# Output projection by halves of the tokens, with the first half's norms beside the second half, in a two-layer FP32 trunk

## The chip, the cores and the metric

One core of a Trainium2 chip runs the whole kernel. The metric is the device time of one execution in microseconds, as the median of several. Five engines work on their own queues and wait for each other through semaphores: TensorE (PE; matmuls and weight loads), VectorE (DVE), ScalarE (ACT), GpSimd (POOL) and SyncE (SP, which only issues DMAs here). Each engine works its instructions off in order.

## The reference

A trunk of two layers over 1024 tokens of width 1024, in FP32. The changed part is what stands between an attention and the up projection of the feed-forward, twice, and the first steps of that:

```python
a = attention_output @ w_o                       # (1024, 1024) @ (1024, 1024)
x = x + rmsnorm(a, g_attn_post[layer])
h = rmsnorm(x, g_ffn_pre[layer])
u = h @ w_up                                     # 1024 -> 2 * 2816
u = causal_conv3(u) + conv_b                     # per channel, over tokens
gate, val = split(u)
f = (silu(gate) * val) @ w_down
x = x + rmsnorm(f, g_ffn_post[layer])
```

## The kernel before

**Layout and precision.** Everything lies transposed: 128 channels on the partitions, tokens along the row. A `128x1024` tile is 128 channels of all tokens, and a *half* is 512 of its columns, so 512 tokens; `half_of(t, k, half)` is such a half of tile k. The width of 1024 makes KT = 8 tiles, 2816 hidden channels make HT = 22 hidden tiles. Every FP32 product is made of three matmuls in fp32r: with each operand split into a high part (a cast) and a low part (the rest), W·X is hi·hi + hi·lo + lo·hi. The weights' parts are made by GpSimd (`split`, two instructions, for the attention's weights; `item` for those of the feed-forward), the activations' by ScalarE (high) and VectorE (low). A product of 128 channels for 512 tokens over eight input tiles is 24 matmuls and fills one PSUM bank; there are eight banks.

**Output projection** (`out_product` on each engine). Units are pairs of weight tiles; for each unit (128 output channels) TensorE makes both token halves, in banks 0 to 3 (`pair_of_units`). VectorE copies each bank to `a`, ScalarE squares it, VectorE adds the square to `ss` (L1754). Loops (`Fori`) run over pairs of units. GpSimd splits a unit's weights when TensorE is through with the ones in their place.

**Norms behind it.** `a_stats` sums `ss` over the partitions by a matmul with ones (L852); ScalarE makes 1/rms with Ln and Exp (L1166, L1168). `x_norm(1)` scales each half tile (L1551), adds it to `x` (L1555, two of three of them on GpSimd, `norm_help`, L718), ScalarE squares it (L1211) and TensorE sums 16 squares (`x_stats`, L845). Then `blocks` makes the feed-forward's input: scaling (L1534), high part (L1175), low part (L1529). `x` is spilled to memory by ScalarE's queue since the room is needed.

**The feed-forward.** Hidden tiles 0 and 1 are plain: products g0, g1, v0, v1 (gate or value, token half 0 or 1), in banks 0 to 3 for both tiles (`plain`, L1080 to L1082). From tile 2 on seven half-size products P1 to P7 stand for eight (Strassen's scheme in Winograd's form; `product`, L1109 to L1111), on sums of weights (S1 to S4, GpSimd) and sums of blocks of the input (T1 to T4), which VectorE makes once in the head of the feed-forward (`sums_of` L1777, `sum_rests` L1783; ScalarE's `sum_tops`, L1186). They use banks 0 to 3; the down projection (`down`, L1127 to L1129) uses banks 4 to 7, and VectorE adds its tiles to `a` (`add`, L1824 for the first hidden tile, L1827). The convolution is one step on ScalarE (`tap`, L1425) and two on VectorE (`conv_tile`, L1804 and L1807); then comes silu (L1429), the product with the value (L1813), and the two parts of `hid` (L1431, L1817).

**What sets the order.** The order on each engine is written out; `STEPS` is TensorE's (`tensor_steps`), `ITEMS` GpSimd's (`weight_items`), and `plan_ring` gives each item one of five places, the one that comes free first. Before, TensorE's order in the head is: plain tile 0 as g0, v0, g1, v1; tile 1 as g0, g1, v0, v1; P1 and P2 of tile 2; the eight down tiles of hidden tile 0; P6, P5, P7, P4 and so on. P1 and P2 write the banks that the convolutions of tile 1 read, and wait for these.

## Time and profile before

| what | us |
|---|---|
| median of 3 runs (2713.6 to 2719.74) | 2714.56 |
| the profiled execution | 2718.21 |
| its span, first to last instruction | 2716.4 |
| TensorE busy in it (matmuls) | 2493.6 |
| VectorE busy in it | 1967.2 |
| mean granted clock of TensorE | 0.967 of full |

The profile is of one execution. Times count from the start of its span. The end of a matmul is modelled, so neighbouring ones overlap on paper; the distance between two starts is the reliable number. "Idle before" an instruction is followed by what ended it. PEclk is the granted clock of TensorE as a share of the full 2.4 GHz; at the lower of its two levels, 1.2 GHz, it is 0.50.

### The profile page before, as it was taken

Reading aid. Unit: us, or ns where it says so; the run is one execution under the profiler, and the core shown is the slowest. Engines: PE = TensorE matmul, PEld = TensorE weight load, DVE = VectorE, ACT = ScalarE, POOL = GpSimd, SP = SyncE. Lnnn points to the kernel's source line nnn. Section 1 sums busy time; section 2 is a strip of 40 time slices with the busy share of each in tenths; the row PEclk is TensorE's granted clock in tenths of the full one; section 3 lists DMA queues with packets and bytes.
Section 4 is the critical chain, followed back from the end, with each engine's and each line's share of the span. In section 5 each row is a group of like instructions: output and inputs, shape, how many; then the busy total and the mean of one; then the engine's idle time right before and its main releaser. Section 6 shows DMA issues by size and latency. Waiting matters only on the chain.

```text
span 2716.4 us, 31720 instructions
## 1 busy us (share of the span) xinstructions
PE 2493.6 (92%) x11964; PEld 1971.9 (73%) x11964; DVE 1967.2 (72%) x2181; ACT 827.7 (30%) x1409; POOL 1490.1 (55%) x1153
## 2 busy tenths in 40 slices
PE   7999999879999999996899999979889999999994
PEld 4688888557777777773577787857467777777772
DVE  4466674586888878889766677653687888788878
ACT  3344442241111111113346565651331111111112
POOL 4231212446888888884431323112537888888883
PEclk9999999999999999998999999979989999999997
DMA  3121223111111111113211213042211111111112
GB/s 133 48 76 63 70 94 149 68 62 47 47 47 55 62 47 47 55 40 144 66 49 45 70 61 86 20 154 93 75 50 47 47 55 57 53 47 48 53 55 116
DMA packets 48928, 183.52 MB, mean 68 GB/s; under 512 B 5648, under 2 KB 6160, under 8 KB 45072
## 3 DMA queue, kind: packets, MB, share of 16 engines
q1 hardware_dynamic: 36880, 140.53, 16.1%
q10 hardware_dynamic: 11904, 41.05, 3.9%
q8 instruction: 93, 1.52, 0.2%
q14 instruction: 51, 0.42, 0.0%
HBM read 138.04 MB, written 29.36 MB: 62 GB/s over the span
## 4 chain that ended last, share of the span: by engine, by line
PE 74%; DVE 16%; ACT 4%; issue 2%; DMA 2%; SPq 1%; ACTq 0%; POOL 0%; POOLq 0%; DVEq 0%
PE ps L1109 9%; PE ps L1110 9%; PE ps L1111 9%; PE ps L1127 6%; PE ps L1129 5%; PE ps L1128 5%; PE ps L975 3%; PE ps L873 3%; PE ps L874 3%; PE ps L875 3%; PE ps L947 2%; DVE a L1551 2%; PE ps L949 2%; PE ps L948 2%; PE ps L1012 2%
## 5 line engine op out<-in xcount | busy, mean ns | idle before, releaser
L1827 DVE TENSOR_TENSOR a<-a,ps 128x1024 f32<-128x1024 f32 x336 | 409.2, 1220 | 173.4 <-PE ps L1129 165.7
L702 POOL CAST w_hi<-w_raw 128x1024 fp32r<-128x1024 f32 x62 | 68.2, 1100 | 648.9 <-PE ps L949 275.3
L785 POOL TENSOR_TENSOR ring<-w_raw,ring 128x512 fp32r<-128x512 f32 x216 | 315.8, 1462 | 17.3
L1425 ACT ACTIVATE cy<-cx,cv 128x1024 f32<-128x1024 f32 x80 | 99.7, 1246 | 718.7 <-DVE cx L1798 718.7
L1127 PE MATMUL ps<-hid,ring 128*128 128x512 f32 x704 | 294.1, 418 | 14.7 <-DVE a L1827 13.5
L783 POOL CAST ring<-w_raw 128x512 fp32r<-128x512 f32 x216 | 176.9, 819 | 235.6 <-PE ps L1129 100.0
L1129 PE MATMUL ps<-hid,ring 128*128 128x512 f32 x704 | 277.1, 394 | 0.0
L1128 PE MATMUL ps<-hid,ring 128*128 128x512 f32 x704 | 276.9, 393 | 0.0
L1109 PE MATMUL ps<-h,ring 128*128 128x512 f32 x640 | 253.3, 396 | 22.1 <-DVE cy L1807 22.1
L1110 PE MATMUL ps<-h,ring 128*128 128x512 f32 x640 | 252.2, 394 | 0.0
L1111 PE MATMUL ps<-h,ring 128*128 128x512 f32 x640 | 252.0, 394 | 0.0
L1127 PEld LDWEIGHTS ps<-hid,ring 128*128 128x128 f32 x704 | 132.5, 188 | 101.1 <-DVE a L1827 64.8
L1798 DVE TENSOR_TENSOR cx<-cx,ps 128x512 f32<-128x512 f32 x280 | 186.9, 680 | 21.8 <-PE ps L1111 13.2
L1109 PEld LDWEIGHTS ps<-h,ring 128*128 128x128 f32 x640 | 122.1, 191 | 49.5 <-issue 24.0
L1129 PEld LDWEIGHTS ps<-hid,ring 128*128 128x128 f32 x704 | 132.9, 189 | 29.9
L704 POOL TENSOR_TENSOR w_lo<-w_raw,w_hi 128x1024 fp32r<-128x1024 f32 x62 | 151.9, 2449 | 5.0
L785 POOL TENSOR_TENSOR ring<-raw_d,ring 128x512 fp32r<-128x512 f32 x88 | 147.2, 1673 | 7.1
L1128 PEld LDWEIGHTS ps<-hid,ring 128*128 128x128 f32 x704 | 133.1, 189 | 20.3
L783 POOL CAST ring<-raw_d 128x512 fp32r<-128x512 f32 x88 | 132.9, 1510 | 26.4 <-PE ps L1082 11.2
L873 PE MATMUL ps<-h,w_hi 128*128 128x512 f32 x352 | 139.8, 397 | 8.3 <-POOL h L723 4.3
L1804 DVE SCALAR_TENSOR_TENSOR cy<-cx,cv,cy 128x1023 f32<-128x1023 f32 x80 | 145.8, 1823 | 0.0
L1111 PEld LDWEIGHTS ps<-h,ring 128*128 128x128 f32 x640 | 122.1, 191 | 26.1
(229 smaller groups left out, 6517.0 us busy)
## 6 DMA issues: line engine op xcount, KB each, us to landing
w_raw<-in_W SPq DMA_DIRECT2D x150, 512.0 KB, 3.5
raw_d<-in_W SPq DMA_DIRECT2D x44, 512.0 KB, 3.5
h<-o_dram ACTq DMA_DIRECT2D x2, 6144.0 KB, 21.0
x_dram<-x ACTq DMA_DIRECT2D x6, 2048.0 KB, 7.2
x<-x_dram SPq DMA_DIRECT2D x2, 4096.0 KB, 12.9
dsw<-draw SPq DMA_DIRECT2D x64, 128.0 KB, 2.3
o_dram<-most SPq DMA_DIRECT2D x6, 1024.0 KB, 4.2
o_dram<-dost SPq DMA_DIRECT2D x6, 1024.0 KB, 4.7
```

Of the source, the lines that this page charges most:

```text
L704: pool.tensor_tensor(w_lo[:, slot, :], w_raw[:, slot, :], w_hi[:, slot, :].bitcast(F32), ALU.subtract).then_inc(w_split, 1)
L783: pool.tensor_copy(half_of(at_, 0, 0), raw[name]).then_inc(item_hi, 1)
L785: pool.tensor_tensor(half_of(at_, 0, 1), raw[name], half_of(at_, 0, 0).bitcast(F32), ALU.subtract).then_inc(item_ready, 1)
L873: pe.matmul(out, wh, xh, start=k == 0, stop=False)
L1109: pe.matmul(out, wh, xh, start=k == 0, stop=False)
L1110: pe.matmul(out, wh, xl, start=False, stop=False)
L1111: last = pe.matmul(out, wl, xh, start=False, stop=k == KH - 1)
L1127: pe.matmul(out, wh, xh, start=True, stop=False)
L1128: pe.matmul(out, wh, xl, start=False, stop=False)
L1129: last = pe.matmul(out, wl, xh, start=False, stop=True)
L1798: dve.tensor_tensor(dst, src, up_bank(n, product), ALU.add).then_inc(c_sum, 1)
L1827: dve.tensor_tensor(a[:, f, :], a[:, f, :], src, ALU.add).then_inc(acc_done, 1)
```

## The change

The projection goes over the first 512 tokens with all eight weight tiles, then over the second 512 with all eight again, so that each weight tile is loaded and split twice (`U_WO = 2 * KT`, and the host lays `w_o` out twice). It uses two banks in turn. The loops are written out. The first norm, the addition to `x`, the second norm and the blocks of the first half (`out_norms` on ScalarE, `new_x` and `blocks` on VectorE) are placed among the steps of the projection's second half; those of the second half come behind it. The 1/rms values stay in the PSUM banks where the sums were made, and so do the scaled tiles on their way; the blocks of the first half are made in PSUM and ScalarE copies them to `a` as well (`b_kept`). All additions to `x` are VectorE's. TensorE's sums are placed between units and, for the second half (`STAT_PLACES`), inside the plain products.

In the feed-forward, TensorE makes the first token half of both plain tiles, then the second half of both; tile 1 uses banks 4 to 7 (`bank(4 * n + ...)`). The weights of tile 1 go to room in `h` (`BESIDE`) instead of the ring. P6 and P5 of tile 2 are moved ahead of the down tiles of tile 0; those are copied to `a` by ScalarE (`first_sum`) instead of VectorE. The order of the convolutions and sums on VectorE and ScalarE changes with it.

```diff
-U_WO = KT
+U_WO = 2 * KT
...
+    out = [("up", n, c) for half in "01" for n in range(PLAIN) for c in ("g" + half, "v" + half)]
     for n in range(PLAIN, HT):
         ups, tiles = [("up", n, c) for c in PRODUCTS], [("dn", n - 1, f) for f in range(KT)]
         if n == PLAIN:
-            first = [("up", n, "P1"), ("up", n, "P2")]
-            out += first + [("dn", m_, f) for m_ in range(n - 1) for f in range(KT)]
-            ups = [u for u in ups if u not in first]
+            out += [("up", n, c) for c in ("P1", "P2", "P6", "P5")] + [("dn", 0, f) for f in range(KT)]
+            ups = [("up", n, c) for c in ("P7", "P4", "P3")]
         if n == HT - 1:
             out += ups + tiles
         else:
...
-    free = {r: (-1 if r < RING - 1 else -2, None) for r in range(RING)}
+    free = {r: (n - RING, None) for n, r in enumerate((4, 0, 2, 1, 3))}
     slot, after = {}, {}
     for it in ITEMS:
+        if it[0] == 1 and it[1] in BESIDE:
+            continue
...
+        STAT_PLACES = {(0, 1, KT - 1): (0, 1), (1, 0, 0): (1, 2), (1, 0, 4): (2, 4), (1, 1, 0): (4, 6), (1, 1, 3): (6, 7),
+                       (1, 1, 6): (7, KT)}
...
+                    if n <= PLAIN:
+                        sp.wait_ge(item_ready, item_count(layer, n - 1, "G2"))
+                        load_ffn(layer, n, "G")
                         sp.wait_ge(item_ready, item_count(layer, n - 1, "V2"))
                         load_ffn(layer, n, "V")
...
                 u0, ch = UNIT0[name], CH[name]
-                for u in range(2):
-                    split(u, u0 + u, before[u])
-                with pool.Fori(1, KT // 2) as q:
-                    free = pairs_free(ch, q - 1)
-                    for u in range(2):
-                        split(u, u0 + 2 * q + u, free[u])
-                return pairs_free(ch, KT // 2 - 1)
+                for u in range(U_WO):
+                    split(u % 2, u0 + u, before[u] if u < 2 else (proj_done, ch + u - 1))
+                return [(proj_done, ch + U_WO - 1), (proj_done, ch + U_WO)]
...
-                pe.wait_ge(proj_out, CH[name])
-                pair_of_units(UNIT0[name], CH[name], True, None)
-                with pe.Fori(1, KT // 2) as q:
-                    pair_of_units(UNIT0[name] + 2 * q, CH[name] + 4 * q, False, None)
+                u0, ch = UNIT0[name], CH[name]
+                for half in range(2):
+                    for t_ in range(KT):
+                        n = KT * half + t_
+                        pe.wait_ge(w_split, u0 + n + 1)
+                        pe.wait_ge(proj_out, ch + n - 1 if n >= 2 else ch)
+                        for k in range(KT):
+                            wh, wl = blk(n % 2, k)
+                            xh, xl = half_of(h, 2 * k, half), half_of(h, 2 * k + 1, half)
+                            pe.matmul(bank(n % 2), wh, xh, start=k == 0, stop=False)
+                            pe.matmul(bank(n % 2), wh, xl, start=False, stop=False)
+                            last = pe.matmul(bank(n % 2), wl, xh, start=False, stop=k == KT - 1)
+                        last.then_inc(proj_done, 1)
+                        if n == KT:
+                            pe.wait_ge(ss_add, SQ0[name] + KT)
+                            a_sum(0)
+                        elif n in (KT + 2, KT + 3):
+                            x_sums(2 * layer + 1, 0, 3 * (n - KT - 2), 3 * (n - KT - 1))
+                        elif n == KT + 4:
+                            x_sums(2 * layer + 1, 0, 6, KT)
...
+                    out = bank(4 * n + 2 * v + half)
+                    if (n, part) == (0, "g0"):
+                        pe.wait_ge(proj_out, CH[f"wo{layer}"] + U_WO)
+                        pe.wait_ge(b_kept, KT * (layer + 1))
                     for k in range(KT):
+                        if (n, part, k) == (0, "g0", 6):
+                            pe.wait_ge(b_lo, 2 * KT * layer + KT)
+                            pe.wait_ge(ss_add, SS[2 * layer])
+                            a_sum(1)
+                        if half == 0 and (n, v, k) in STAT_PLACES:
+                            x_sums(2 * layer + 1, 1, *STAT_PLACES[n, v, k])
...
-                    if n > 0 or f >= 2:
-                        pe.wait_ge(acc_done, down_count(layer, n, f) - 2)
+                    if n == 0 and f < 2:
+                        pe.wait_ge(conv_done, conv_count(layer, 1, f))
+                    elif KT * n + f < KT + 2:
+                        pe.wait_ge(acc_first, KT * layer + KT * n + f - 1)
+                    else:
+                        pe.wait_ge(acc_done, acc_count(layer, n, f) - 2)
                     f4 = f % 4
...
+            def out_norms(layer):
+
+                ch, c0, na, nx = CH[f"wo{layer}"], SQ0[f"wo{layer}"], 2 * layer, 2 * layer + 1
+
+                def square(n):
+                    act.wait_ge(proj_out, ch + n + 1)
+                    if n >= 2:
+                        act.wait_ge(ss_add, c0 + n - 1)
+                    act.activation(half_of(sq, 1, n % 2), half_of(a, n % KT, n // KT), ACT.Square).then_inc(a_sq, 1)
...
+                def x_square(i):
+                    half, k = NORM_TILES[i]
+                    act.wait_ge(f_new, 16 * layer + i + 1)
+                    if i >= 2:
+                        act.wait_ge(x_stat, nx * 16 + i - 1)
+                    act.activation(half_of(sq, 0, i % 2), half_of(x, k, half), ACT.Square).then_inc(x_sq, 1)
+
...
+                def block_parts(i):
+
+                    half, k = NORM_TILES[i]
+                    src = half_of(a, k, half) if half else block_bank(i)
+                    act.wait_ge(b_f, 2 * KT * layer + i + 1)
+                    act.activation(direct(half, k)[0], src, ACT.Copy).then_inc(b_hi, 1)
+                    if half == 0:
+                        act.activation(half_of(a, k, half), src, ACT.Copy).then_inc(b_kept, 1)
+
+                for n in range(KT):
+                    square(n)
+                rstd_a(0)
+                square(KT)
+                for n, squares in enumerate(((0, 1), (2, 3, 4), (5, 6, 7))):
+                    for i in squares:
+                        x_square(i)
+                    if n == 2:
+                        spill(0)
+                    square(KT + n + 1)
+                square(KT + 4)
+                rstd_x(0)
+                for n, tiles_ in enumerate(((0, 1, 2), (3, 4, 5), (6, 7))):
+                    for i in tiles_:
+                        block_parts(i)
+                    square(KT + 5 + n)
+                rstd_a(1)
+                for i in range(KT, 2 * KT):
+                    x_square(i)
+                spill(1)
+                rstd_x(1)
+                for i in range(KT, 2 * KT):
+                    block_parts(i)
...
+                def first_sum(f):
+
+                    act.wait_ge(dn_done, down_count(layer, 0, f))
+                    for c in (("T1", "T3") if f < KH else ("T4",)):
+                        act.wait_ge(t_rest[c], KH * layer + f % KH + 1)
+                    act.activation(a[:, f, :], bank(4 + 2 * (f % 2), 2), ACT.Copy).then_inc(acc_first, 1)
...
                 sum_tops(layer, "T2")
-                gate_and_split(1)
+                sum_tops(layer, "T1")
+                gate(1)
+                sum_tops(layer, "T3")
+                sum_tops(layer, "T4")
+                for f in range(KT - 1):
+                    first_sum(f)
                 bank_copy(layer, PLAIN)
+                first_sum(KT - 1)
+                hid_top(1)
...
+                def copy(n):
+                    dve.wait_ge(proj_done, ch + n + 1)
+                    dve.tensor_copy(half_of(a, n % KT, n // KT), bank(n % 2)).then_inc(proj_out, 1)
+
+                def add_square(n):
+                    dve.wait_ge(a_sq, q0 + n + 1)
+                    dve.wait_ge(ss_add, c0 + n)
+                    dve.tensor_tensor(half_of(ss, 0, n // KT), half_of(ss, 0, n // KT), half_of(sq, 1, n % 2),
+                                      ALU.add).then_inc(ss_add, 1)
+
+                def new_x(i):
+                    half, k = NORM_TILES[i]
+                    if k == 0:
+                        dve.wait_ge(a_rstd, 2 * na + half + 1)
+                    if k >= 2:
+                        dve.wait_ge(f_new, 16 * layer + i - 1)
+                    dve.scalar_tensor_tensor(added_bank(half, i), half_of(a, k, half), gain(post, k), bank(4 + half),
+                                             ALU.mult, ALU.mult).then_inc(a_normed, 1)
+                    dve.wait_ge(a_normed, na * 16 + i + 1)
+                    dve.tensor_tensor(half_of(x, k, half), half_of(x, k, half), added_bank(half, i), ALU.add
+                                      ).then_inc(f_new, 1)
...
+                def block(i):
+                    half, k = NORM_TILES[i]
...
+                    dve.scalar_tensor_tensor(half_of(a, k, half) if half else block_bank(i), half_of(x, k, half),
+                                             gain(pre, k), bank(6 + half), ALU.mult, ALU.mult).then_inc(b_f, 1)
...
+                    if half:
+                        dve.wait_ge(b_hi, 2 * KT * layer + i + 1)
+                    else:
+                        dve.wait_ge(b_kept, KT * layer + i + 1)
+                    dve.tensor_tensor(lo, half_of(a, k, half) if half else block_bank(i), hi.bitcast(F32), ALU.subtract
+                                      ).then_inc(b_lo, 1)
+
+                def blocks(i0, i1):
+                    for i in range(i0, i1):
+                        block(i)
+                        if i > i0:
+                            block_rest(i - 1)
+                    block_rest(i1 - 1)
...
+                for n in range(KT):
+                    copy(n)
+                    add_square(n)
+                dve.wait_ge(x_in, X_IN[nx])
+                for t_ in range(KT):
+                    copy(KT + t_)
+                    for i in {0: (0, 1), 1: (2, 3, 4), 2: (5, 6, 7)}.get(t_, ()):
+                        new_x(i)
+                    if 4 <= t_ < 7:
+                        blocks(3 * (t_ - 4), min(3 * (t_ - 3), KT))
+                    add_square(KT + t_)
+                dve.wait_ge(b_kept, KT * (layer + 1))
+                for i in range(KT, 2 * KT):
+                    new_x(i)
+                blocks(KT, 2 * KT)
...
+                    if n == 1:
+                        dve.wait_ge(acc_first, KT * layer + f + 1)
...
                 conv_tile(0, 0)
                 sums_of("T1")
                 conv_tile(0, 1)
+                product(0)
                 sums_of("T2")
-                product(0)
+                hid_tail(0)
                 sums_of("T3")
-                hid_tail(0)
+                conv_tile(1, 0)
+                conv_tile(1, 1)
+                sum_rests("T2")
                 sum_rests("T1")
                 sums_of("T4")
-                conv_tile(1, 0)
                 sum_rests("T3")
                 sum_rests("T4")
-                conv_tile(1, 1)
-                sum_rests("T2")
-                add(0, 0)
                 product(1)
-                for f in range(1, KT):
```

## Rows read from the trace of the kernel before

**Rows 1.** The page: TensorE to GpSimd busy; a group of VectorE; the weight loads.

```profile
PE 2493.6 (92%) x11964; PEld 1971.9 (73%) x11964; DVE 1967.2 (72%) x2181; ACT 827.7 (30%) x1409; POOL 1490.1 (55%) x1153
...
L1798 DVE TENSOR_TENSOR cx<-cx,ps 128x512 f32<-128x512 f32 x280 | 186.9, 680 | 21.8 <-PE ps L1111 13.2
...
w_raw<-in_W SPq DMA_DIRECT2D x150, 512.0 KB, 3.5
```

**Rows 2.** Timeline of TensorE: start us, us, line, tiles, [idle before].

```profile
426.18 0.47 PE L873 MATMUL ps<-h,w_hi 128*128 128x512 f32 x1 [0.98 <-issue]
...
516.19 1.98 PE L852 MATMUL ps<-ss,ones 128*128 128x512 f32 x4 [2.69 <-DVE ss L1754]
...
535.79 1.13 PE L845 MATMUL ps<-sq,ones 128*128 128x512 f32 x2 [1.01 <-ACT sq L1211]
...
547.79 0.47 PE L1080 MATMUL ps<-h,ring 128*128 128x512 f32 x1 [1.54 <-DVE h L1529]
...
600.53 0.77 PE L1109 MATMUL ps<-h,ring 128*128 128x512 f32 x1 [4.93 <-DVE cy L1807]
...
611.92 0.77 PE L1109 MATMUL ps<-h,ring 128*128 128x512 f32 x1 [5.93 <-DVE cy L1807]
...
616.75 0.41 PE L1111 MATMUL ps<-h,ring 128*128 128x512 f32 x1
...
629.58 0.39 PE L1109 MATMUL ps<-t_r,ring 128*128 128x512 f32 x1
...
635.04 0.39 PE L1109 MATMUL ps<-x_r,ring 128*128 128x512 f32 x1
...
1937.23 3.32 PE L852 MATMUL ps<-ss,ones 128*128 128x512 f32 x4 [2.69 <-DVE ss L1754]
...
2055.80 0.39 PE L1109 MATMUL ps<-x_r,ring 128*128 128x512 f32 x1
```

**Rows 3.** Chain that ended last, 505 to 570 us: start us, us, what.

```profile
517.35 0.70 ACT rstd_a L1166
...
518.81 0.76 DVE a L1551
...
519.60 0.69 DVE x L1555
```

**Rows 4.** Timeline of VectorE in the head of the first feed-forward.

```profile
547.57 0.74 DVE L1534 SCALAR_TENSOR_TENSOR a<-x,par,rstd_x 128x512 f32<-128x512 f32 x1
...
548.84 0.74 DVE L1534 SCALAR_TENSOR_TENSOR a<-x,par,rstd_x 128x512 f32<-128x512 f32 x1
...
569.74 1.28 DVE L1804 SCALAR_TENSOR_TENSOR cy<-ps,cv,cy 128x1023 f32<-128x1023 f32 x1 [4.45 <-ACT cy L1425]
...
593.51 2.48 DVE L1777 TENSOR_TENSOR a<-a,cx 128x512 f32<-128x512 f32 x4
...
600.30 8.97 DVE L1783 TENSOR_TENSOR x_r<-a,x_r 128x512 fp32r<-128x512 f32 x8
```

**Rows 5.** Timeline of VectorE in the output projections.

```profile
460.81 2.57 DVE L1754 TENSOR_TENSOR ss<-ss,sq 128x512 f32<-128x512 f32 x1 [0.87 <-ACT sq L1411]
...
466.26 0.69 DVE L1754 TENSOR_TENSOR ss<-ss,sq 128x512 f32<-128x512 f32 x1 [0.88 <-ACT sq L1411]
...
513.65 0.69 DVE L1750 COPY a<-ps 128x512 f32 x1 [3.18 <-PE ps L875]
...
1934.69 0.69 DVE L1750 COPY a<-ps 128x512 f32 x1 [3.09 <-PE ps L875]
```

**Rows 6.** Timeline of GpSimd in the first output projection.

```profile
459.31 1.04 POOL L702 CAST w_hi<-w_raw 128x1024 fp32r<-128x1024 f32 x1
...
460.43 2.40 POOL L704 TENSOR_TENSOR w_lo<-w_raw,w_hi 128x1024 fp32r<-128x1024 f32 x1
```

**Rows 7.** Timeline of ScalarE: two 512-column casts of block parts.

```profile
545.06 1.15 ACT L1175 ACTIVATE h<-a 128x512 fp32r<-128x512 f32 x2
```

**Rows 8.** One window: window, length, busy us of the engines, PEclk, DMA.

```profile
600.00:620.00 20.00, 13.54 (x37) 10.01 (x38) 15.56 (x17) 1.87 (x3) 9.09 (x8) 0.67 0.03 11
```

183 lines of the change are left out of this document (83 added, 100 removed).

## The prediction, made before the change was run

> **What bounds the kernel now.** I read the page's busy table first: TensorE is busy for 92% of the span [rows 1], so what is left to win is where it waits. The timeline of TensorE shows where, around the output projection [rows 2]. The projection starts at 426.18. Each of its 16 unit-halves takes 5.44 us (24 matmuls of 0.227), as 629.58 to 635.04 shows for the same number of matmuls. The last one is copied out at 513.65, and the first feed-forward matmul starts at 547.79. Between them there is a chain over both token halves: Ln and Exp of the first norm, scaling, adding to x, squares, the second norm [rows 3]. Three further waits follow in the head of the feed-forward: 4.93 and 5.93 us ahead of the products P1 and P2 of hidden tile 2, which need banks that VectorE frees late, and the pace of the first product, one block part in 1.27 us (547.57 to 548.84 in [rows 4]) where its three matmuls need 0.68.
>
> I measure everything from A, the start of the projection's second half: 426.18 + 8 x 5.44 = 469.7. The mark at the end is the start of P7 of hidden tile 2: by then both versions have done the same products (eight plain ones, P1, P2, P6, P5, the down projection of tile 0), although in another order. Before, P7 starts at 635.04, A + 165.3. In layer 1 the stretch from the last copy to P7 is 1934.69 to 2055.80, 121.1 us, against 121.4 in layer 0 [rows 2, 5]: one sum does for both layers.
>
> **TensorE's own work from A to P7.** Eight unit-halves 43.5; 18 sums by the ones matrix (two of the first norm, 16 of the second) at 0.85, the difference of a group of two sums (1.98) and one (1.13) [rows 2], 15.3; eight plain products 43.5; P1, P2, P6, P5 10.9; eight down tiles of six matmuls 10.9. Together 124.1, before and after: the change removes no matmul. Before, 41.2 us of the 165.3 are waits and half clock. The question is what the waits come to after.
>
> **Projection by halves.** The weights are loaded and split 16 times instead of 8. A split is 1.04 us of cast and 2.40 of subtraction [rows 6], 3.6 in a unit of 5.44, and it may start when the unit two before has ended: ready 1.8 us early. A load lands in 3.5 us [rows 1]; split to split of one slot is 3.6 + 3.5 = 7.1 of 10.9 us. I cost both at nothing. If that cover failed (splits at 5.5), it would be some 0.1 us for each unit. In the second half nine sums lie between units: the half ends at A + 51.2, and 0.4 more for two squares that wait for their buffer: A + 51.6.
>
> **The first half's norms beside it.** VectorE does everything in order, with one copy (0.69, [rows 5]) per unit. Scaling and adding one tile takes 1.48 (518.81 to 519.60, then 0.69 [rows 3]); the new ones read PSUM, and with a PSUM input an add of 512 columns takes 0.68 and a scaling of 1023 columns 1.28, so 0.7 for 512 [rows 1, 4]. The eight tiles fit between the copies of units 8, 9 and 10 and end at A + 23. The second norm is ready 1.4 us (Ln and Exp, 517.35 to 518.81 [rows 3]) after the sum that ends at 35.3: A + 37.1. Then VectorE is late. Three tiles of blocks take 5.8 us: two operations of 0.7 each, and ScalarE's two copies (1.15 [rows 7]) to wait for. The addition of squares behind them is a two-SBUF-input one beside a split: such a one takes 2.57 instead of 0.69 [rows 5, 6]. So the copy of unit 13 is at 45.0, that of 14 at 52.3, and that of 15, behind two tiles, at 58.0. The last copy is due at 51.9. The first plain product waits for it: it starts at 58.9, **7.3 us late** after A + 51.6. From both sides: 4.5 if no addition meets a split, 10 if the eight scalings into PSUM, which no row shows, cost the 1.0 us of a contended one. I take 7.3, as the nearest PSUM rows are uncontended.
>
> The 280 adds with one input in PSUM have a mean of 0.68 us, in a span of which GpSimd works 55% [rows 1]: they don't wait for it. By the Trainium skill's page "SBUF — State Buffer", section "Who interferes with whom", an instruction of VectorE with at most one SBUF input does not contend with GpSimd and one with two does; the trace agrees, and by this page the new tiles would cost 7.3 and not 10.
>
> **The second half's chain under four products.** The sum of squares of half 1 needs the late copy and goes into the first product after six blocks; the first norm is ready at A + 67.7, the eight tiles take 8 x 1.48 until 79.6. The first product ends at 67.6; TensorE needs the first square ahead of the last part of the second (72.4), and has it at 70.2. The other squares too are there in time. The fourth product ends at 90.8; the second norm comes after the last sum in it (89.4 + 0.3 + 1.4) and the first block part 2.3 later: product g1 starts at 93.4, **2.6 late**, and runs at 1.27 for each part, **4.2** more than its 5.4, to 103.0. The three later products end at 119.3, P1 and P2 at 124.8: their waits of 4.93 and 5.93 are gone, since the plain products of tile 1 use banks 4 to 7 and the first convolutions have long been done.
>
> **The head of the feed-forward.** VectorE, from 103.0: two convolutions of two 1.28 operations, sums T1, T2, T3 (2.5 per four, somewhat more beside GpSimd [rows 4]), the product and the low part of tile 0, two convolutions; it gets to the rests of T2 at A + 128.1. P6 starts at 128.8, **4.0 late**; bounds 1 and 8, for the two rates of such groups (2.48 for four, 8.97 for eight [rows 4]). The down tiles of tile 0 are then copied by ScalarE, which first has the tops of T4 to do (until 138.3): their third tile starts at 139.7, **2.6 late**; the six others lose **0.5** against ScalarE's 1.15 per 1024 columns [rows 7], and P7 waits **1.0** for the bank copy behind the last one. SP's queue waits for both spills of x ahead of the loads for tile 2; the second is issued behind the last square of x, some A + 87, so these loads land by A + 105, and GpSimd has split the first when P1 starts at 119.3: nothing. That cover is some 10 us.
>
> **The clock.** After the waits of 4.93 and 5.93 the granted clock was at its lower level, 1.2 GHz of 2.4 (0.67 on average of 600 to 620 [rows 8]): 11 matmul steps between 611.92 and 616.75 took 0.44 instead of 0.227, 2.4 us lost [rows 2]. A wait of 2.69 us cost it in layer 1 (two sums in 3.32 us) and not in layer 0 (1.98) [rows 2]. I take 2.4 us behind the wait of 7.3 and half of that behind the one of 4.0: **3.6**; bounds 0 and 10 (all four waits of 2.6 and more).
>
> **Sum.** 7.3 + 0.4 + 2.6 + 4.2 + 4.0 + 2.6 + 0.5 + 1.0 = 22.6, with the clock 26.2. 124.1 + 26.2 = A + 150.3, against A + 165.3: 15.0 us less for each layer, 30.0 together. Behind P7 nothing is late: product, split and down tiles of tile 1 come with 2 us to spare, and the steady loop is untouched. The profiled execution took 2718.21 us around its span of 2716.4; it is 3.65 above the median of 2714.56. From 2718.21 this gives 2688.2, from the median **2684.6**.
>
> **Rivals.**
> - *Most of it hides* (0.16). The late copy at 4.5, the rests at 1, the other waits at a half (5.5), no loss of clock: 11.4 us of waits, 29.8 us less per layer, 2655 at best; half of that way, 22.4 per layer, 2670. For it: the uncontended rows. Against it: VectorE has over 20 us of work from 37.1 on, and in strict order.
> - *Little is left* (0.14). Waits at their dear ends: late copy 10, rests 8, clock 8: 11.1 us more, so 3.9 us less per layer, 2707; half of that way 2696. For it: 8.97 us for eight rests beside GpSimd. 0.06 of this lies within 0.2%, which is about what a measurement of this kernel can tell from no change.
> - *Slower: the clock stays down* (0.08). After the late copy the four products and nine sums (29.4 us of work) run at 1.2 GHz to the end: 29.4 more, 2.4 of it already counted. That is 27.0 - 15.0 = 12.0 us per layer slower than before, 2739. It decides from 15.0 us of work at the lower clock beyond what I count. Against it: the clock came back within the 4.83 us of dense work at 611.92.
> - *The overlap doesn't come about*: VectorE, in order, delays the copies so much that TensorE waits inside the projection. The copy of unit 13 is at 45.0 and is due at 46.2 (unit 15), a margin of 0.5 with the copy itself; each us beyond is one lost, but it also moves the last copy, so it is the same cost as in "little is left".
>
> **Chances and range.** Forecast, 2674 to 2697: 0.62. Faster by over 0.2%: 0.62 + 0.16 + 0.08 = 0.86; within 0.06; slower 0.08. The range takes in half the way to the first rival's best and a little more, 2665, and the second's 2707: it leaves out the best of the one, no change, and slower.
>
> **What the profile after would show.** TensorE: no wait over 1 us inside the projection; one of 7 after it, released by the copy of the last unit; one of 2.6 at g1 of tile 0, which is then paced at 1.27; no wait at P1 and P2, one of 4 at P6, one of 2.6 in the down tiles. First unit of the second half to P7: 150. Wrong it would be by a VectorE operation into PSUM far from 0.7, by more contended rests, or by a lower clock that outlasts 5 us.

## The result: 1.5% faster, and the profile after

The changed kernel takes 2675.1 us (median of four runs, 2668.7 to 2680.9), the kernel before beside it 2716.5: a ratio of 0.985 (0.982 to 0.987). That is 41 us less; 30 were forecast, 2684.6 from the median of the kernel before. The profiled execution is the longest of the four, 2680.91 around a span of 2679.1.

Busy times on the page of the changed kernel, with the two groups that answer to [rows 1]: TensorE does the same work as before; VectorE is busy 21 us less, ScalarE 22 and GpSimd 30 more, and sixteen more weight loads are issued.

```profile
PE 2487.5 (93%) x11964; PEld 1974.9 (74%) x11964; DVE 1946.4 (73%) x2185; ACT 850.1 (32%) x1441; POOL 1520.2 (57%) x1153
...
L1949 DVE TENSOR_TENSOR cx<-cx,ps 128x512 f32<-128x512 f32 x280 | 187.0, 681 | 25.8 <-ACT cx L1243 14.5
...
w_raw<-in_W SPq DMA_DIRECT2D x166, 512.0 KB, 3.2
```

TensorE's timeline answers to [rows 2]: the projection's first matmul, the first of the feed-forward (g0), the sum of half 1's squares in it, g1, the first matmul after g1 (of v1), P6, the first down tile, P7.

```profile
427.88 0.47 PE L1101 MATMUL ps<-h,w_hi 128*128 128x512 f32 x1 [0.98 <-issue]
...
526.72 0.80 PE L1139 MATMUL ps<-h,ring 128*128 128x512 f32 x1 [3.22 <-DVE a L1841]
...
533.75 0.59 PE L876 MATMUL ps<-ss,ones 128*128 128x512 f32 x1
...
561.81 0.47 PE L1139 MATMUL ps<-t_r,ring 128*128 128x512 f32 x1 [2.23 <-DVE t_r L1878]
...
571.57 0.40 PE L1139 MATMUL ps<-t_r,ring 128*128 128x512 f32 x1
...
597.84 0.76 PE L1168 MATMUL ps<-t_r,ring 128*128 128x512 f32 x1 [4.30 <-DVE t_r L1934]
...
604.91 0.39 PE L1190 MATMUL ps<-hid,ring 128*128 128x512 f32 x1
...
617.00 0.47 PE L1168 MATMUL ps<-x_r,ring 128*128 128x512 f32 x1 [0.79 <-issue]
```

From the projection's start to P7 are 189.1 us, against 208.9 before [rows 2]; in layer 1 191.3 against 210.1. TensorE's waits from 471 to 640 us (who waits, for whom, total, times, longest):

```profile
PE ps L1168 <- DVE t_r L1934: 4.3, 1, 4.3
PE ps L1139 <- DVE a L1841: 3.2, 1, 3.2
PE ps L1139 <- DVE t_r L1878: 2.5, 2, 2.2
PE ps L1139 <- DVE h L1878: 1.0, 2, 0.7
PE ps L1168 <- issue: 0.8, 1, 0.8
```

These are the waits that the prediction named (P6, last copy, g1, P7); the 4.93 and 5.93 ahead of P1 and P2 are gone, and the down tiles have none. A, the start of the second half, is 471.4 here, and P7 comes at A + 145.6, forecast 150.3.

### The profile page after: what moved, and what is told of

It is laid out like the page before. It is cut to its first block, busy times and chain, and to the rows that moved or that the text cites. A ratio compares the mean times of both kernels' runs of the same rounds, so it can differ in the third digit from the quotient of the medians.

```text
span 2679.1 us, 31652 instructions
## 1 busy us (share of the span) xinstructions
PE 2487.5 (93%) x11964; PEld 1974.9 (74%) x11964; DVE 1946.4 (73%) x2185; ACT 850.1 (32%) x1441; POOL 1520.2 (57%) x1153
## 4 chain that ended last, share of the span: by engine, by line
PE 76%; DVE 13%; ACT 4%; issue 3%; DMA 2%; POOL 1%; SPq 1%; ACTq 0%; POOLq 0%; DVEq 0%
PE ps L1168 9%; PE ps L1169 9%; PE ps L1170 9%; PE ps L1190 6%; PE ps L1192 5%; PE ps L1191 5%; PE ps L1011 3%; PE ps L983 2%; PE ps L985 2%; PE ps L984 2%; PE ps L1101 2%; PE ps L1102 2%; PE ps L1103 2%; PE ps L1028 2%; PE ps L1048 2%
## 5 line engine op out<-in xcount | busy, mean ns | idle before, releaser
L733 POOL CAST w_hi<-w_raw 128x1024 fp32r<-128x1024 f32 x78 | 85.0, 1089 | 788.2 <-PE ps L985 274.3
L815 POOL TENSOR_TENSOR ring<-w_raw,ring 128x512 fp32r<-128x512 f32 x208 | 301.7, 1450 | 16.6
L813 POOL CAST ring<-w_raw 128x512 fp32r<-128x512 f32 x208 | 183.2, 881 | 209.4 <-PE ps L1192 91.2
L1168 PE MATMUL ps<-h,ring 128*128 128x512 f32 x640 | 249.2, 389 | 0.0
L1169 PE MATMUL ps<-h,ring 128*128 128x512 f32 x640 | 249.0, 389 | 0.0
L1170 PE MATMUL ps<-h,ring 128*128 128x512 f32 x640 | 249.0, 389 | 0.0
L735 POOL TENSOR_TENSOR w_lo<-w_raw,w_hi 128x1024 fp32r<-128x1024 f32 x78 | 190.5, 2443 | 6.2
L1168 PEld LDWEIGHTS ps<-h,ring 128*128 128x128 f32 x640 | 120.3, 188 | 25.2
L1169 PEld LDWEIGHTS ps<-h,ring 128*128 128x128 f32 x640 | 120.2, 188 | 25.0
L1170 PEld LDWEIGHTS ps<-h,ring 128*128 128x128 f32 x640 | 120.2, 188 | 25.0
```

The lines of the kernel that those rows point to most:

```text
L735: pool.tensor_tensor(w_lo[:, slot, :], w_raw[:, slot, :], w_hi[:, slot, :].bitcast(F32), ALU.subtract).then_inc(w_split, 1)
L813: pool.tensor_copy(hi, raw[name]).then_inc(item_hi, 1)
L815: pool.tensor_tensor(lo, raw[name], hi.bitcast(F32), ALU.subtract).then_inc(item_ready, 1)
L1168: pe.matmul(out, wh, xh, start=k == 0, stop=False)
L1169: pe.matmul(out, wh, xl, start=False, stop=False)
L1170: last = pe.matmul(out, wl, xh, start=False, stop=k == KH - 1)
```

## The experiments

The mark throughout is the time from the projection's first matmul to P7, read from each run's TensorE timeline, in layer 0 and layer 1; it leaves out what varies ahead of the projection, whose start lies between 423.5 and 431.3 in runs that have the same instructions there. Ratios are against the kernel before, run on the same chip; the first four runs shared a chip, then the next four, then three, then one. Each mark is of one execution. In executions with the same instructions up to there, the way from the start of g0 to the sum in it took 5.5 to 7.0 us, by how long the granted clock stayed at its lower level; so a difference of some 1.5 us at one mark alone says little.

| run | median us | ratio (95%) | layer 0 | layer 1 |
|---|---|---|---|---|
| before | | | 208.9 | 210.1 |
| changed again | 2675.2 | 0.9827 (0.9812 to 0.9841) | 188.5 | 191.2 |
| serial norms | 2699.5 | 0.9917 (0.9904 to 0.9931) | 199.2 | 201.5 |
| copy first | 2666.4 | 0.9798 (0.9784 to 0.9811) | 183.9 | 187.5 |
| fill wait | 2680.3 | 0.9848 (0.9833 to 0.9862) | 188.4 | 191.3 |
| early sums | 2670.6 | 0.9814 (0.9798 to 0.9829) | 187.1 | 188.3 |
| early rests | 2675.9 | 0.9837 (0.9823 to 0.9850) | 191.3 | 194.1 |
| three edits | 2663.6 | 0.9791 (0.9776 to 0.9807) | 184.5 | 187.2 |
| squares in PSUM | 2675.8 | 0.9838 (0.9822 to 0.9853) | 187.1 | 191.1 |
| second serial | 2679.9 | 0.9855 (0.9838 to 0.9871) | 190.9 | 192.3 |
| tight sums | 2655.9 | 0.9771 (0.9756 to 0.9786) | 177.6 | 179.3 |
| tight and rests | 2659.8 | 0.9783 (0.9768 to 0.9798) | 178.4 | 180.7 |
| both serial | 2710.6 | 0.9966 (0.9954 to 0.9978) | 205.1 | 208.4 |

**Changed again.** 

> The changed kernel itself, as the yardstick for the runs beside it. Both theories expect 0.985 of the kernel before (0.982 to 0.988), which is 2675 us where the kernel before takes 2716.

It repeats the result, and shows what one execution differs from the next by.

### Where the gain comes from

**Serial norms.** TensorE's side; ScalarE's and VectorE's orders follow it (all squares and copies first, then eight tiles, then eight blocks). The wait for `b_kept` moves from g0 to v0, which alone uses a bank of the blocks.

```diff
-                        if n == KT:
+                        if n == 2 * KT - 1:
                             pe.wait_ge(ss_add, SQ0[name] + KT)
                             a_sum(0)
-                        elif n in (KT + 2, KT + 3):
-                            x_sums(2 * layer + 1, 0, 3 * (n - KT - 2), 3 * (n - KT - 1))
...
+                            x_sums(2 * layer + 1, 0, 0, KT)
```

> The head of the FFN by token halves and the weights split twice are kept, but the first half's sums of squares, additions and blocks come behind the projection's last unit instead of beside it; nothing of the computation changes. Theory (the overlap is what gains): after the last unit TensorE has to wait for the sum (0.7), rstd (2.0), eight norm tiles at 1.39 (11.1), the last square and stat (1.3), rstd (2.0) and the first block (1.9), some 19 us where the changed kernel waits 3.2, less the 5.4 us of its eight norm sums, which TensorE no longer does between units but in these waits; the first product is then paced by blocks at 1.9 against 0.68 a tile, up to 8 more. Per layer 13 to 22 us longer, 26 to 44 in all: 2700 to 2720 us where the changed kernel takes 2675, so most or all of the gain is gone. Rival (the head by halves gains by itself, and the overlap little): less than 8 us per layer, under 2691 us in all.

Measured: 24 us more in all, 10.8 and 10.3 at the marks; half of the gain stays. That lies between the two, just under the theory's price (26 to 44 in all) and well over the rival's (under 16). TensorE's waits between the projection's start and P7:

```profile
PE ps L1137 <- DVE h L1869: 5.4, 4, 4.1
PE ps L888 <- ACT sq L1476: 4.7, 4, 3.9
PE ps L1166 <- DVE t_r L1924: 4.3, 1, 4.3
PE ps L1137 <- DVE t_r L1869: 3.0, 4, 2.2
PE ps L876 <- DVE h L1869: 1.5, 1, 1.5
```

The chain that the overlap hides now shows as waits. The first product, whose pacing by blocks I had counted at up to 8 more, takes 8.7 us from its start to the sum in it, 3.0 more than in the changed kernel.

**Second serial.** The other overlap alone is undone.

```diff
                     if (n, part) == (0, "g0"):
                         pe.wait_ge(proj_out, CH[f"wo{layer}"] + U_WO)
                         pe.wait_ge(b_kept, KT * (layer + 1))
+                        pe.wait_ge(b_lo, 2 * KT * layer + KT)
+                        pe.wait_ge(ss_add, SS[2 * layer])
+                        a_sum(1)
+                        x_sums(2 * layer + 1, 1, 0, KT)
...
-                        if (n, part, k) == (0, "g0", 6):
-                            a_sum(1)
-                        if half == 0 and (n, v, k) in STAT_PLACES:
-                            x_sums(2 * layer + 1, 1, *STAT_PLACES[n, v, k])
```

> The other overlap of the change is undone: the second half's sums of squares and of tiles come ahead of the FFN's first product instead of inside the first four products; the first half's norms stay beside the projection's second half. Nothing of the computation changes. Theory (both overlaps gain, and together they are the whole of the change's gain): TensorE waits some 19 us for the second half's chain (the sum, rstd 2.0, eight tiles at 1.39, the last square and stat 1.3, rstd 2.0; the same chain as in the run of the serial norms), its stats (7.0 us) lie in the wait, the wait ahead of the second half's first product and its pace (2.2 and some 4 us) go away: 6 to 12 us per layer longer, 12 to 24 in all, 2687 to 2699 us where the changed kernel takes 2675. With the 24 us of the other overlap that makes 36 to 48 of the 47 gained. Rival (only one of the overlaps counts, and the rest comes from the shorter sums of rests beside GpSimd or from the weights): less than 4 us per layer.

Measured: 2.5 and 1.1 us at the marks, some 5 to 8 in all, and the ratio's interval overlaps that of the changed kernel: the rival's size. TensorE's timeline:

```profile
528.53 2.04 PE L876 MATMUL ps<-ss,ones 128*128 128x512 f32 x2 [5.08 <-DVE ss L1844]
534.19 9.45 PE L888 MATMUL ps<-sq,ones 128*128 128x512 f32 x14 [3.61 <-ACT sq L1476]
543.90 1.12 PE L888 MATMUL ps<-sq,ones 128*128 128x512 f32 x2 [0.26 <-ACT sq L1476]
544.46 0.79 PE L1137 MATMUL ps<-h,ring 128*128 128x512 f32 x1
```

g0 starts 116.6 after the projection's start and not 98.8, 17.8 later. But the sums (7 us) now lie in that time, and ahead of the second half's products nothing waits or paces. The overlap as made let g0 start 18 us sooner and paid most of that back, in the sums between the products and in the wait and pace of g1.

**Both serial.** The two edits together; the wait for `b_kept` stays ahead of g0.

> Both overlaps undone at once: all of the first half's norms behind the projection's last unit, and all of the second half's ahead of the FFN's first product. The order of the products (first halves first, P6 and P5 ahead of the down tiles) and the weights split twice stay. Nothing of the computation changes. Undone singly they cost 10.8 and 2.5 us from the projection's start to P7 in layer 0, where the kernel before takes 20.4 us more than the changed one. Theory (the second overlap is worth little only because in the changed kernel it keeps waits of its own, and what the two do not explain comes of the products' order): 14 to 18 us per layer over the changed kernel, 203 to 206 us from the projection's start to P7, 2703 to 2712 us in all, still 0.2 to 0.5% under the kernel before. Rival (the overlaps are the whole gain, and not additive): 209 us or more in layer 0, no faster than the kernel before.

Measured: 205.1 in layer 0, 2710.6 us in all, 0.34% under before (0.22 to 0.46): the theory. So of the 20.4 us that layer 0 gained, the overlaps hold 16.6 together, more than the 10.8 and 2.5 they cost singly. In layer 1 it is 17.2 of 18.9. The other 3.8 and 1.7 stay in this kernel, which differs from the one before by the products' order (no wait ahead of P1 and P2, one of 4.4 ahead of P6), and by all else that the change holds: the weights split twice, the loops written out, the norms by halves, the additions to `x` all on VectorE, the first sums on ScalarE. None of these was tried apart.

### The wait behind the projection

**Copy first.**

```diff
-                    if 4 <= t_ < 7:
-                        blocks(3 * (t_ - 4), min(3 * (t_ - 3), KT))
+                    if t_ in (4, 5):
+                        blocks(3 * (t_ - 4), 3 * (t_ - 3))
+                    if t_ == KT - 1:
+                        blocks(6, KT)
...
-                        pe.wait_ge(proj_out, CH[f"wo{layer}"] + U_WO)
+                        pe.wait_ge(proj_out, CH[f"wo{layer}"] + U_WO - 1)
+                    if (n, part) == (0, "v0"):
                         pe.wait_ge(b_kept, KT * (layer + 1))
...
-                        if (n, part, k) == (0, "g0", 6):
+                        if (n, part, k) == (0, "g0", 7):
```

> VectorE's copy of the last unit goes ahead of the last two blocks instead of behind them and the addition of unit 14's squares; the first product of the FFN waits for the copies of all units but the last, and no longer for ScalarE's copies of the blocks (the second product does). Nothing of the computation changes. Theory of the prediction (the late copy is a wait of its own, and the clock falls behind it): the wait of 3.2 us ahead of the first product goes to under 1, and with it the 2.8 us that the lower clock cost behind it; 4 to 6 us per layer, 8 to 12 us in all, 2663 to 2667 us where the changed kernel takes 2675. Rival (the wait is hidden by slack further on, because the chain of the second half's norms sets the start of the second half's products): VectorE's own chain is not shorter, the time moves into the wait ahead of the second half's first product, and the total changes by under 3 us.

Measured: 4.6 and 3.7 us at the marks, 9 in all: the wait was on the path, and so its cause, VectorE's order, is shown. (The edit also takes the wait for `b_kept` from g0, but in the changed kernel ScalarE's last copy of a block was done by 524.4, before VectorE's copy at 525.98.) VectorE here copies the last unit and then makes the two blocks:

```profile
523.11 1.09 DVE L1847 TENSOR_TENSOR ss<-ss,sq 128x512 f32<-128x512 f32 x1 [0.70 <-ACT sq L1459]
524.35 0.69 DVE L1842 COPY a<-ps 128x512 f32<-128x512 f32 x1
524.96 1.41 DVE L1869 SCALAR_TENSOR_TENSOR ps<-x,par,ps 128x512 f32<-128x512 f32 x2
```

**Fill wait.**

```diff
+                        pe.wait_ge(proj_out, CH[f"wo{layer}"] + U_WO - 1)
+                        for k in range(6):
+                            pe.matmul(bank(0), ones[:, :], half_of(ss, 0, 0), start=True, stop=True)
                         pe.wait_ge(proj_out, CH[f"wo{layer}"] + U_WO)
```

> Six more products of ones with the squares' sums, some 0.47 us each, are put into the wait ahead of the FFN's first product, into the bank which that product clears; nothing of the computation changes. They are work without use, in time in which TensorE stood still. Theory (the lower clock behind the wait comes of TensorE standing still): the granted clock stays at its higher level behind the wait and 2.8 us per layer come back, if the six end by the time the copy is there; 5 us in all, 2670 us where the changed kernel takes 2675. Rival (the lower clock there has another reason, or its cost is hidden by the norms' chain further on): no change, or 1 to 2 us longer where the six products end late.

The window 524 to 528 (length, busy us of each engine, PEclk, DMA) of the changed kernel run beside it:

```profile
524.00:528.00 4.00, 3.94 (x11) 3.13 (x12) 1.08 (x2) 0.63 (x1) 3.92 (x4) 0.60 0.34 125
```

The same window of this run:

```profile
524.00:528.00 4.00, 4.00 (x14) 2.32 (x13) 1.63 (x2) 0.63 (x1) 3.84 (x4) 1.00 0.34 131
```

With TensorE kept busy the clock stayed up: the stillness is what lowered it. The way from g0's start to the sum inside it fell from 5.69 to 4.53 us. But the six products took 4.75 us, 1.5 more than the wait and not the 2.8 that were expected of six, so the marks are unchanged, as the rival has it. The lower clock cost 1.2 us here; in the profiled execution of the result the same way took 7.03, 2.5 more than at full clock. The median is 5 us above the changed kernel's, though the intervals overlap; the marks do not show where, and I leave that open.

### The second half's start, and the head

**Squares in PSUM.**

```diff
+                    out = bank(6 + n % 2) if n < KT else half_of(sq, 1, n % 2)
-                    act.activation(half_of(sq, 1, n % 2), half_of(a, n % KT, n // KT), ACT.Square).then_inc(a_sq, 1)
+                    act.activation(out, half_of(a, n % KT, n // KT), ACT.Square).then_inc(a_sq, 1)
```

> In the projection's first half the squares go to a PSUM bank instead of SBUF, so that VectorE's addition of them has one operand in SBUF instead of two; nothing of the computation changes. Theory (the addition took 2.77 us there and 0.68 to 1.1 in the second half because with two operands in SBUF it waits until GpSimd's instruction of that moment has ended, and in the first half it always starts 0.17 us behind GpSimd's 2.39 us one): the additions take 0.7 us each, and, since VectorE waits for the next unit anyway, the time of the kernel stays within 0.2% of the changed kernel's. Rival (the 2.77 us are the engine's own for that addition, or come of the moment's traffic): they stay near 2.8 us. The Trainium skill (SBUF — State Buffer, Who interferes with whom) states that a VectorE instruction with one operand in SBUF or none does not contend with GpSimd and one with two does; by that the additions take 0.7 us too.

Measured: 0.69 each, and no change of the whole. The same addition on VectorE's timeline in the changed kernel:

```profile
456.79 2.77 DVE L1846 TENSOR_TENSOR ss<-ss,sq 128x512 f32<-128x512 f32 x1 [0.70 <-ACT sq L1458]
```

GpSimd's timeline there:

```profile
456.62 2.39 POOL L735 TENSOR_TENSOR w_lo<-w_raw,w_hi 128x1024 fp32r<-128x1024 f32 x1
```

And the addition in this run:

```profile
460.30 0.69 DVE L1848 TENSOR_TENSOR ss<-ss,ps 128x512 f32<-128x512 f32 x1 [0.67 <-ACT ps L1459]
```

beside the same instruction of GpSimd:

```profile
460.16 2.39 POOL L735 TENSOR_TENSOR w_lo<-w_raw,w_hi 128x1024 fp32r<-128x1024 f32 x1
```

In the changed kernel GpSimd's instruction ends at 459.01 and the addition 0.55 later. It is not slowed by a factor: it stands until the other has ended. So its length is about what is left of GpSimd's instruction, plus 0.55 us.

**Early sums.**

```diff
-        STAT_PLACES = {(0, 1, KT - 1): (0, 1), (1, 0, 0): (1, 2), (1, 0, 4): (2, 4), (1, 1, 0): (4, 6), (1, 1, 3): (6, 7),
-                       (1, 1, 6): (7, KT)}
+        STAT_PLACES = {(0, 1, KT - 1): (0, 1), (1, 0, 0): (1, 2), (1, 0, 2): (2, 3), (1, 0, 4): (3, 4),
+                       (1, 0, 6): (4, 5), (1, 1, 0): (5, 6), (1, 1, 1): (6, 7), (1, 1, 2): (7, KT)}
```

> The eight sums of the second half's squares are put earlier and more evenly into TensorE's third and fourth product (the last of them behind the second step of the fourth product, not behind its sixth), so that the second half's rstd and blocks begin while the fourth product still runs. Nothing of the computation changes; there are two groups of sums more, some 0.4 us each. Theory of the prediction (the start of the second half's products is late by the norms' chain: a wait of 2.2 us, then products paced by the blocks at 1.27 a tile against 0.68, and a lower clock behind the wait): last sum some 4 us earlier, no wait ahead of the second half's first product, and that product some 6 us instead of 9 to 10 long; 4 to 7 us per layer, 8 to 14 in all: 2661 to 2667 us where the changed kernel takes 2675. Rival (the time is given back further on, since VectorE's sums of tiles, the weights' loads behind the spills or the wait ahead of P6 come later by as much): the wait ahead of P6 grows from 4.3 to 8 us or more, and the total changes by under 3 us.

Measured: 1.3 and 2.9 us at the marks, some 4 in all, between theory and rival. The wait ahead of g1 is gone and P6's is 4.3 as before, so nothing was given back there; but the last sum came only 1.6 us earlier against the projection's start, not 4 (four k steps of 0.68, less 1.1 for a longer stretch of lower clock in g0). A sum costs 0.88 wherever it stands, alone or in a pair.

**Early rests.**

```diff
                 conv_tile(1, 0)
-                conv_tile(1, 1)
                 sum_rests("T2")
                 sum_rests("T1")
+                conv_tile(1, 1)
                 sums_of("T4")
```

> VectorE makes the rests of T2 and T1 ahead of the second tile's second convolution instead of behind it (2.5 us of work passed); nothing of the computation changes. Theory (the wait of 4.3 us ahead of P6 is VectorE's own chain, and nothing is behind it that is as late): the wait falls to 1.8 us, with the clock behind it 2.5 to 3.5 us per layer, 5 to 7 in all: 2668 to 2670 us where the changed kernel takes 2675. Rival (the next thing is as late: the tops of T4, the first sums of the down tiles or the split weights of P7): the time goes into waits of the down tiles or of P7, under 1 us per layer.

Measured: 2.9 us longer at both marks, 1 to 3 in all: the rival's mechanism, a wait that comes up in the down tiles, but with a loss where it had a small gain. P6, its second step, and the third down tile:

```profile
590.72 0.47 PE L1168 MATMUL ps<-t_r,ring 128*128 128x512 f32 x1 [1.84 <-DVE t_r L1934]
592.32 0.80 PE L1168 MATMUL ps<-t_r,ring 128*128 128x512 f32 x1 [0.38 <-DVE t_r L1934]
...
605.17 0.79 PE L1190 MATMUL ps<-hid,ring 128*128 128x512 f32 x1 [4.04 <-ACT a L1543]
```

And VectorE's sums of T4, for which ScalarE's tops and behind them its first sums wait; in the changed kernel they took 2.49:

```profile
598.31 5.07 DVE L1928 TENSOR_TENSOR a<-a,cx 128x512 f32<-128x512 f32 x4
```

They have two inputs in SBUF and now run beside GpSimd, which works without a gap from 598.55 to 602.83. The wait of the down tiles, which I had forecast and which did not come, exists: it was hidden by P6's.

**Three edits** (copy first, early sums, early rests).

> The copy of the last unit first, the sums of the second half's squares earlier, and the rests of T2 and T1 earlier, together. Nothing of the computation changes. Theory (the three waits stand one behind another on TensorE's path, so that their gains add): 4.4 (as measured) + 5.5 + 2.5 us per layer, 25 in all: 2650 us where the changed kernel takes 2675 (2645 to 2656). Rival (one of them is the same slack seen twice): 2658 to 2664 us.

Measured: 2663.6, in the rival's range, and no better at the marks than copy first alone. P6 waits 3.6 in layer 0, the third down tile 3.5: the early rests undo what the early sums bring, as they do when the two single runs are added up.

**Tight sums** (copy first, and this).

```diff
+        STAT_PLACES = {(0, 1, KT - 1): (0, 1), **{(1, 0, k): (k + 1, k + 2) for k in range(KT - 1)}}
```

> The copy of the last unit first, as before, and the sums of the second half's squares one behind each step of the third product, the last behind its seventh. Nothing of the computation changes. The run with the earlier sums showed that a sum costs TensorE 0.88 us wherever it stands, and that ScalarE's squares waited for it. Theory (VectorE's blocks of the second half set the start and the pace of the second half's first product): the blocks begin some 6.4 us earlier against the fourth product's end than in the changed kernel, the wait is gone, the pacing shrinks to the last tiles; 4.4 for the copy and 4 to 5 for the sums per layer, 17 to 19 in all: 2656 to 2659 us where the changed kernel takes 2675. Rival (what the second half's start gains is lost ahead of P6 or in the down tiles): 2662 us or more.

Measured: 2655.9 us, 10.8 and 11.9 less at the marks: the theory. (Of the 11.9, 1.0 lies ahead of the edits: the projection of layer 1 begins at the lower clock, which in this execution ended sooner.) The last sum stands at 118.2 after the projection's start, against 127.9. TensorE's waits:

```profile
PE ps L1168 <- DVE t_r L1936: 4.3, 1, 4.3
PE ps L1100 <- issue: 1.0, 1, 1.0
PE ps L1168 <- issue: 0.8, 1, 0.8
PE ps L875 <- DVE ss L1846: 0.5, 1, 0.5
```

Of the waits over 1 us, the one ahead of P6 is all that is left. This is the fastest kernel of the study, 0.977 (0.976 to 0.979) of the one before.

**Tight and rests.**

```diff
                 sum_rests("T1")
+                sum_rests("T3")
+                conv_tile(1, 1)
                 sums_of("T4")
-                sum_rests("T3")
...
                 for f in range(KT - 1):
                     first_sum(f)
+                    if 1 <= f < KH:
+                        sum_tops(layer, "T4", f - 1, f + (f == KH - 1))
```

> As the run with the tight sums, and in addition VectorE makes the rests of T2, T1 and T3 ahead of the second tile's second convolution, and ScalarE makes T4's tops one by one between the first sums of the down tiles. Nothing of the computation changes. The run with the earlier rests showed the wait ahead of P6 fall by 2.4 us and a wait of 4.0 us come up in the third down tile, for ScalarE's first sums, which stood behind T4's tops. Theory (that second wait is only their order): the wait ahead of P6 1.8 to 3.6 us, none over 1 us in the down tiles, 2 to 3 us per layer, 4 to 6 in all less than the run with the tight sums: 2651 to 2655 us. Rival (VectorE is the bound of this stretch, so that any order leaves the same sum of waits): no change against the tight sums, or waits of the same size in later down tiles.

Measured: 0.8 and 1.4 us longer at the marks than the tight sums (1.1 of the 1.4 being the same luck at the start of the projection), the intervals overlap: the rival. The wait of 4.0 in the down tiles did go (0.31 is left), so it was the order. In layer 0, P6 still waits 3.6, and P6 with P5 takes 8.0 us instead of 7.2. VectorE has no gap there from 559.33 to the rests of T2, and its sums of T2 and T3, which stand ahead of the edit, meet GpSimd, where they did not in the changed kernel (2.48 and 2.49):

```profile
571.07 4.00 DVE L1931 TENSOR_TENSOR cx<-a 128x512 f32<-128x512 f32 x4
...
576.12 4.00 DVE L1931 TENSOR_TENSOR a<-a 128x512 f32<-128x512 f32 x4
```

In layer 1 they don't meet, and the wait did fall as forecast, from 4.3 to 1.8 and 0.7 ahead of the second step. But P6 with P5 then took 9.3 us instead of 7.1, with a wait in it and a stretch of lower clock that lasted longer. The window 1974 to 1978 of layer 1 (the last but two is PEclk):

```profile
1974.00:1978.00 4.00, 4.00 (x10) 3.10 (x10) 4.00 (x8) 0.23 (x1) 1.81 (x1) 0.51 0.00 0
```

So neither of the two orders that were tried gained. That VectorE's load is the bound of this stretch is not shown; in layer 1 the second wait and the lower clock took the time back.

## Why the prediction was right, and where its terms were off

Its sum, beside what the profiled execution shows from A on:

| step | forecast | measured |
|---|---|---|
| second half of the projection | 51.6 | 52.1 |
| wait for the last copy | 7.3 | 3.2 |
| four products and nine sums, clock in it | 31.9 | 32.9 |
| wait at g1 | 2.6 | 2.2 |
| g1, paced | 9.6 | 9.8 |
| three products | 16.3 | 16.4 |
| P1, P2 | 5.5 | 5.6 |
| wait at P6 | 4.0 | 4.3 |
| P6, P5, clock in it | 6.6 | 7.1 |
| eight down tiles | 14.0 | 11.3 |
| P7 | 1.0 | 0.8 |
| sum | 150.3 | 145.6 |

(The terms are rounded. They are of layer 0; in layer 1, where the projection starts at the lower clock, P7 comes at A + 147.7.)

The 2675.1 lie 1.1 us inside the lower end of the range, 2674 to 2697, and two of the four executions, 2668.7 and 2673.8, lie below it. The mechanism came out as forecast, but that the median fell inside the range owes something to luck; the gain is 41 us and not 30.

Two terms are off: together 6.8 too much, while all others together are 2.1 too little. **The late copy** was mis-sized at 7.3, outside my bounds of 4.5 to 10. The mechanism is as forecast (copy first removed it); the size is not. I priced the addition behind blocks at the 2.57 of a row [rows 5]. The three took 0.84, 1.13 and 1.06, because that row's length was a matter of when GpSimd's instruction had begun. VectorE's timeline of the changed kernel:

```profile
519.87 1.13 DVE L1846 TENSOR_TENSOR ss<-ss,sq 128x512 f32<-128x512 f32 x1
```

and GpSimd's:

```profile
519.15 1.29 POOL L815 TENSOR_TENSOR ring<-w_raw,ring 128x512 fp32r<-128x512 f32 x1
```

GpSimd ends at 520.44, the addition 0.56 later. The rest of the term: three blocks took 5.0 and not 5.8. The sum was not made from its own prices either: from 37.1 on, blocks at 5.8, 5.8 and 3.9, each with an addition of 2.57 and two of them with a copy of 0.69 ahead, put the last copy at A + 61.7 and the wait at some 11, above my own bound; I wrote 58.0. It came at A + 54.6. The lower bound, "if no addition meets a split", was still too high for that. That scalings into PSUM would cost 0.7 held (1.42 for two).

**The down tiles** were forecast 2.7 too long: T4's tops ended at 605, before the third tile asked. VectorE was not held up in the sums of T4 and the rests of T3 and T4 (4.91 for the eight rests against 8.97 [rows 4]). The run with the early rests shows the term as 4.0, where the sums of T4 are held up.

The clock was rightly placed, behind the copy and behind the wait at P6: it cost about 2.5 and 1.6 in this execution, forecast 2.4 and 1.2, and 1.2 at the first in another. It also fell behind the wait at g1 (granted 0.50 from 564 to 566 us), where VectorE set the pace anyway. Costs of the weights split twice, of the loads behind the spills and of P1 and P2: nothing, as forecast. Of the rivals, "most of it hides" came nearer than I thought, by the two terms above; "little is left" and the clock that stays down did not happen; inside the projection no wait over 1 us came up.

## What to carry to other kernels

Where an in-order engine serves a copy that TensorE waits for and a chain that nobody waits for yet, put the copy first: here that was worth as much as a fifth of the whole change. An overlap is worth what its own chain leaves: the second one gained 1 to 3 us per layer as made, and with the sums placed at each step (and the copy first), so that ScalarE waits 0.9 us for the buffer of a square and not up to 3.0, 6 to 7 more. And before moving work ahead of the wait that the list shows, look for the wait that it hides.

## What the hardware showed that I had not expected

A VectorE operation with two inputs in SBUF waits for the end of GpSimd's instruction of that moment (2.77 us with 2.22 left of GpSimd's, 1.13 with 0.57 left). The other way round, a string of them can keep GpSimd out for the whole string: a cast that takes 0.61 us alone took 8.34 beside sums and rests that ran without a gap from 601.82 on, and ended 0.5 behind the last of them. It took 7.37 at the same place in layer 1, and 8.25 in the run with the tight sums. GpSimd's timeline in the changed kernel:

```profile
602.40 8.34 POOL L813 CAST ring<-w_raw 128x512 fp32r<-128x512 f32 x1 [6.59 <-PE ps L1170]
```

VectorE's, the last two groups of the string:

```profile
604.22 4.91 DVE L1934 TENSOR_TENSOR x_r<-a,x_r 128x512 fp32r<-128x512 f32 x8
609.04 1.23 DVE L1964 TENSOR_TENSOR cy<-cy 128x1024 f32<-128x1024 f32 x1
```

It is not always so. In the same kernel, four sums that began while GpSimd was busy with a string of its own took turns with it and needed 5.67 us instead of 2.49:

```profile
575.59 5.67 DVE L1928 TENSOR_TENSOR a<-a 128x512 f32<-128x512 f32 x4
```

And in the run with the early rests a cast that began 0.24 behind VectorE's first sum (at 598.31) was let in after that sum:

```profile
598.55 0.91 POOL L813 CAST ring<-raw_d 128x512 fp32r<-128x512 f32 x1 [0.80 <-PE ps L1170]
```

What decides between the two is open.

The Trainium skill's page "SBUF — State Buffer", section "SBUF: two separate sides", says that of a VectorE operation with two SBUF inputs and a GpSimd operation that reads SBUF, the one that starts first has the shared ports for its whole instruction, and that the other blocks fully. The single additions agree (2.77 and 1.13 us). It speaks of one instruction; the 8.34 us are a whole string. In the changed kernel that was the cheaper outcome: VectorE, for which TensorE waits here, ran at 0.61 a tile.
